# Hybrid decoder trunk, one core: the attention runs without projection work inside it, and the order of work changes at four other places

## The reference

```python
h = rms_norm(x, norm_pre_mix[l])
proj = h @ w_in[l]
p_rwkv, p_nsa, p_swa, p_gate = _split(proj, (RWKV_COLS, NSA_COLS, SWA_COLS, GATE_COLS))
o_rwkv = rwkv7_time_mix(p_rwkv, ...)      # 8 heads of 64, a recurrence over the tokens
o_nsa = nsa_mix(p_nsa, ...)               # compressed, selected and sliding-window branches, 8 heads
o_swa = swa_sink_mix(p_swa, ...)          # window 128, a sink per head
gates = jax.nn.sigmoid(p_gate).reshape(B, T, N_BRANCHES, D)
merged = sum(gates[:, :, i] * (o_i @ w_branch[l, i]) for i in range(3))
x = x + rms_norm(merged @ w_out[l], norm_post_mix[l])
h = rms_norm(x, norm_pre_ffn[l])
f = (silu(h @ ffn_w_gate[l]) * (h @ ffn_w_up[l])) @ ffn_w_down[l]
x = x + rms_norm(f, norm_post_ffn[l])
```

## Time and profile before

| | us |
|---|---|
| median of 3 runs | 1119.35 (1115.24 to 1119.69) |
| profiled execution | 1118.18 |
| its span, first to last instruction | 1116.0 |
| PE busy | 1063.8 (95%) |
| DVE, POOL, ACT busy | 534.5, 505.8, 363.1 |
| granted TensorE clock, mean share of full speed | 0.988 |

### The profile page before, as it was taken

The page is one execution under the profiler, slowest core; times in us unless marked ns, Lnnn a source line. Parts: engine busy times, 40 slices in busy tenths (PEclk is TensorE's granted clock), DMA queues, the critical chain, the costliest instruction groups (busy, mean ns, idle before and its releaser), DMA issues.

```text
span 1116.0 us, 18780 instructions
## 1 busy us (share of the span) xinstructions
PE 1063.8 (95%) x7568; PEld 839.7 (75%) x7568; DVE 534.5 (48%) x909; ACT 363.1 (33%) x708; POOL 505.8 (45%) x428
## 2 busy tenths in 40 slices
PE   5989998999989999999988999999999999999997
PEld 4767777787877667776656877888888888888886
DVE  5774497466465444445544367135445454530004
ACT  4223232321322214444452244444222322221222
POOL 2355544113022347655696544653444444444452
PEclk9999999999999999999998999999999999999999
DMA  7334533002025354221201454812333333333321
GB/s 216 96 89 138 113 88 74 11 13 57 5 59 133 90 123 142 58 58 30 67 20 49 128 174 117 258 40 76 94 94 100 92 109 94 113 95 95 96 93 76
DMA packets 149138, 102.40 MB, mean 92 GB/s; under 512 B 20870, under 2 KB 131728, under 8 KB 149065
## 3 DMA queue, kind: packets, MB, share of 16 engines
q1 hardware_dynamic: 145424, 96.48, 30.0%
q10 hardware_dynamic: 3608, 4.88, 2.0%
q0 software_dynamic: 32, 0.00, 0.0%
HBM read 93.72 MB, written 7.63 MB: 91 GB/s over the span
## 4 chain that ended last, share of the span: by engine, by line
PE 82%; DVE 10%; POOL 3%; issue 1%; ACT 1%; DMA 1%; ACTq 0%; DVEq 0%; POOLq 0%
PE ps L1491 17%; PE ps L1493 15%; PE ps L1492 15%; PE ps L1627 4%; PE ps L1937 4%; PE ps L1938 4%; PE ps L1936 4%; PE ps L1537 3%; PE ps L1788 3%; PE ps L1835 2%; POOL EB L638 1%; DVE XF L1039 1%; PE ps L1858 1%; PE ps L1859 1%; PE ps L1860 1%
## 5 line engine op out<-in xcount | busy, mean ns | idle before, releaser
L577 POOL TENSOR_TENSOR WLO<-WRAW,WHI 128x1024 fp32r<-128x1024 f32 (+1 forms) x129 | 287.7, 2231 | 295.3 <-ACT WHI L690 170.0
L1491 PE MATMUL ps<-HHI,WHI 128*128 128x512 f32 x776 | 319.3, 411 | 8.1 <-DVE GATES L995 5.4
L1492 PE MATMUL ps<-HLO,WHI 128*128 128x512 f32 x776 | 305.5, 394 | 0.0
L1493 PE MATMUL ps<-HHI,WLO 128*128 128x512 f32 x776 | 305.4, 394 | 0.0
L1491 PEld LDWEIGHTS ps<-HHI,WHI 128*128 128x128 f32 x776 | 147.5, 190 | 63.6 <-issue 29.4
L1493 PEld LDWEIGHTS ps<-HHI,WLO 128*128 128x128 f32 x776 | 147.2, 190 | 31.9
L1492 PEld LDWEIGHTS ps<-HLO,WHI 128*128 128x128 f32 x776 | 147.6, 190 | 29.1 <-issue 1.9
L581 POOL CAST WHI<-WRAW 128x256 fp32r<-128x256 f32 (+1 forms) x83 | 48.4, 583 | 192.1 <-PE ps L1493 192.1
L690 ACT ACTIVATE WHI<-WRAW 128x1024 fp32r<-128x1024 f32 (+1 forms) x70 | 63.6, 909 | 161.0 <-PE ps L1493 82.9
L1449 DVE TENSOR_TENSOR FT<-FT 128x512 f32<-128x512 f32 x22 | 51.7, 2348 | 89.0 <-ACT FT L942 89.0
L836 ACT ACTIVATE EB<-EB,MISC 128x257 f32<-128x257 f32 (+5 forms) x96 | 50.7, 530 | 66.7 <-DVE MISC L1337 53.2
(11 more groups left out here) (303 smaller groups left out, 1668.8 us busy)
## 6 DMA issues: line engine op xcount, KB each, us to landing
WRAW<-in_w_in SPq DMA_DIRECT2D x47, 512.0 KB, 4.0
WRAW<-in_w_gate SPq DMA_DIRECT2D x22, 512.0 KB, 3.9
WRAW<-in_w_up SPq DMA_DIRECT2D x22, 512.0 KB, 4.0
WRAW<-in_w_down SPq DMA_DIRECT2D x22, 512.0 KB, 3.9
spilled<-SQ SPq DMA_DIRECT2D x21, 256.0 KB, 2.3
WRAW<-in_w_in SPq DMA_DIRECT2D x16, 256.0 KB, 3.8
WRAW<-in_w_branch SPq DMA_DIRECT2D x32, 128.0 KB, 2.9
WRAW<-in_w_out SPq DMA_DIRECT2D x8, 512.0 KB, 4.2
```

Source lines behind the costliest of these rows:

```text
L577: return pool.tensor_tensor(lo[:, 0:chunks, :], WRAW[:, n % NRAW, 0:chunks, :], hi[:, 0:chunks, :].bitcast(F32), ALU.subtract)
L1491: pe.matmul(dst, WHI[:, s, k, :], hi, start=start, stop=False)
L1492: pe.matmul(dst, WHI[:, s, k, :], lo, start=False, stop=False)
L1493: return pe.matmul(dst, WLO[:, s, k, :], hi, start=False, stop=stop)
```

## The change

- `FILL`: the fill before the first RWKV pass goes from 16 to 20 chunks, the one that opens each pass from 2 to 5, the last before the attention from 4 to 7. No fill is left inside the attention. Behind it come `PT_TAIL`, three fills of one tile each, and the rest. That makes 192 chunks (24 tiles) before and 120 chunks (15 tiles) behind.
- Attention: scores alternate between `R[0]`, `R[1]` and `DB[0]`, `DB[1]`, so they wait for step n - 2; transposes stand three steps behind the scores and PV four; `EB` has four buffers. Before its first step PE waits for the evacuation of the last projection tile. POOL's cutting of weights into pieces is gone; two tiles are prepared before the attention, the others behind it.
- Start: x in four tiles of 128 tokens, three of them ahead of the first weight tile, one between the first two; constants issued by SP and not by ACT; transposes into eight banks; squares summed over the free dimension of x on ACT and DVE, one root and reciprocal of 128x4, spread by diagonals and the ones-matmul; weight tile 1's high part on POOL, weight tile 0's ahead of the copies on ACT. The root's table is the one loaded first.
- `compress_low(0)` stands before `compress_in(1)`, `compress_low(1)` stays.
- Behind the attention one tile is evacuated before each four `OLO` operations.
- Several semaphores are merged into `norm_std`; their waits are the same.

```diff
@@ -136,7 +136,7 @@
-POOL_HI = list(range(NS0 + 4, MERGE0))
+POOL_HI = [1] + list(range(NS0 + 4, MERGE0))
@@ -188,11 +188,11 @@
 FILL = []
-PT_UP = len(FILL); FILL += [4, 4, 8, 8, 16]
+PT_UP = len(FILL); FILL += [4, 4, 8, 8, 20]
 PT_CP = []
 for _cp in range(4):
-    PT_CP.append(len(FILL)); FILL += [2, 4, 4] + [0] * 4 + [1, 1, 1, 1, 1, 4]
-PT_GN = len(FILL); FILL += [3, 6, 6, 6, 4, 4, 8, 8, 4, 4, 4]
+    PT_CP.append(len(FILL)); FILL += [5, 4, 4] + [0] * 4 + [1, 1, 1, 1, 1, 4]
+PT_GN = len(FILL); FILL += [3, 6, 6, 6, 4, 4, 8, 8, 4, 4, 7]
@@ -203,9 +203,9 @@
 NST = len(STEPS)
-PT_ATT = len(FILL); FILL += [2] * NSA_STEPS + [1] * (NST - NSA_STEPS) + [0] * 3
 _ends = np.cumsum([j[3] for j in JOBS[NS0:MERGE0]])
-PT_SPLIT = len(FILL); FILL += [_ends[-1] - sum(FILL)]
+PT_TAIL = len(FILL); FILL += [8, 8, 8]
+FILL += [_ends[-1] - sum(FILL)]
 DONE = []
@@ -214,8 +214,8 @@
 FILLED = np.cumsum(FILL)
-ATT_JOB = NS0 + int(np.sum(_ends - 8 < FILLED[PT_ATT - 1] + 8))
-assert all(j[3] == 8 for j in JOBS[ATT_JOB - 1:MERGE0])
+ATT_JOB = NS0 + int(FILLED[PT_TAIL - 1]) // 8
+assert FILLED[PT_TAIL - 1] % 8 == 0 and ATT_JOB > SW0 + 6
@@ -302,8 +302,8 @@
-    EB = at("EB", 50, [P, 3, 2, T])
-    PTB = at("PTB", 62, [P, 2, 2, T])
+    EB = at("EB", 50, [P, 4, 2, T])
+    PTB = at("PTB", 66, [P, 2, 2, T])
@@ -382,6 +382,9 @@
+    def score_bank(n, g):
+        return (R[g], DB[g])[n % 2]
...
     def out_bank(t, dh):
...
@@ -510,16 +514,28 @@
+    selt = con[0:NH, CON["selT"]:CON["selT"] + 4 * P].rearrange("h (m p) -> h m p", m=4)
...
     block = nc.Block()
...
         def _(sp):
-            for c in range(2):
-                sp.dma_start(XTOK0[:, :, 512 * c:512 * c + 512], x.rearrange("(t p) d -> p t d", p=P)[:, :, 512 * c:512 * c + 512])\
-                    .then_inc((x_in, xtok_in)[c], 16)
+            def x_tile(t):
+                sp.dma_start(XTOK0[:, t, :], x[t * P:(t + 1) * P, :]).then_inc(x_in[t], 16)
...
+            for t in range(3):
+                x_tile(t)
             for n in range(FF0):
-                if n < 2:
-                    sp.wait_ge((x_in, xtok_in)[n], 16)
+                if n == 1:
+                    x_tile(3)
+                if n == 2:
+                    sp.dma_start(HOT[:, :], hot).then_inc(hot_in, 16)
+                    sp.dma_start(SNK, bass.AP(sinks.tensor, 0, [[0, P], [1, NH]])).then_inc(hot_in, 16)
+                    sp.dma_start(MASK[:, :], con[:, NCONP:NCON]).then_inc(hot_in, 16)
+                if n == 3:
+                    sp.dma_start(SELT[0][:, :, :], selt).then_inc(selt_in, 16)
+                    sp.dma_start(WA[0:64, :], w2).then_inc(wsmall_in, 16)
+                    sp.dma_start(WA[64:128, :], a2).then_inc(wsmall_in, 16)
                 if n - 4 in SPILLED:
@@ -588,37 +604,15 @@
-            for n in range(ATT_JOB):
+            for n in range(ATT_JOB + 1):
                 whole_tile(n)
...
-            split = {"at": int(_ends[ATT_JOB - NS0 - 1]), "pieces": 0}
...
-            def split_upto(count):
...
-                while split["at"] < min(count, int(_ends[-1])):
-                    n = NS0 + int(np.sum(_ends <= split["at"]))
...
-                    lo = pool.tensor_tensor(WLO[:, slot_of(n), k:k + 2, :], WRAW[:, n % NRAW, k:k + 2, :],
-                                            WHI[:, slot_of(n), k:k + 2, :].bitcast(F32), ALU.subtract)
...
             pool.memset(ECB[:, :, :, :], 0.0).then_inc(zero_ok, 1)
...
+            whole_tile(ATT_JOB + 1)
...
@@ -638,21 +632,21 @@
-            for n in range(NST + 3):
+            for n in range(NST + 1):
                 if n < NST and STEPS[n][0] == "swa":
-                    pool.wait_ge(p_T, n - 2)
-                    pool.tensor_copy(EB[:, n % 3, :, keys_of(n):keys_of(n) + 1],
+                    pool.wait_ge(p_T, n - 3)
+                    pool.tensor_copy(EB[:, n % 4, :, keys_of(n):keys_of(n) + 1],
                                      NSNK[:, STEPS[n][2]:NH:4].unsqueeze(2)).then_inc(snk_ok, 1)
-                if 1 <= n < NST + 1:
+                if n >= 1:
                     weigh(n - 1)
-                split_upto(int(FILLED[PT_ATT + n]) + 8)
-            split_upto(int(_ends[-1]))
+            for n in range(ATT_JOB + 2, MERGE0):
+                whole_tile(n)
...
                 if u == 2:
-                    pool.wait_ge(xtok_in, 32)
+                    pool.wait_ge(xtok_in, 16)
                     for n in range(8):
@@ -678,40 +672,35 @@
             act.wait_ge(eps_ok, 1)
-            act.activation(MISC[:, 70:72], EPSC, ACT.Square)
+            act.activation(MISC[:, 70:72], EPSC, ACT.Sqrt)
...
                     act.wait_ge(dense_done, slot_free(n))
-                if n == MERGE0:
+                if n in (2, MERGE0):
                     act.wait_ge(w_hi, n)
...
+            def x_square(t):
+                act.wait_ge(x_in[t], 16)
+                act.activation(SQ[:, :, :].rearrange("p a t -> p (a t)"), XTOK0[:, t, :], ACT.Square,
+                               accum_out=XSS[:, t:t + 1]).then_inc(xsq_ok, 1)
...
+            x_square(0)
+            act.wait_ge(xsq_ok, 1)
+            x_square(2)
+            hi_part(0)
             act.wait_ge(prow_ok, 2)
...
                 act.wait_ge(xT_done, k + 1)
-                act.activation(HHI[:, k, :], R[k % 4][:, :], ACT.Identity, scale=par("g_pre_mix", k))
-                if k >= 2:
-                    act.wait_ge(xsum_ok, k - 1)
-                act.activation(SQ[:, k % 2, :], R[k % 4][:, :], ACT.Square).then_inc(xsq_ok, 1)
-                if k == 3:
-                    hi_part(0)
...
-                    act.dma_start(MASK[:, :], con[:, NCONP:NCON]).then_inc(hot_in, 16)
-                    act.dma_start(WA[0:64, :], w2).then_inc(wsmall_in, 16)
-                    act.dma_start(WA[64:128, :], a2).then_inc(wsmall_in, 16)
-                    selt = con[0:NH, CON["selT"]:CON["selT"] + 4 * P].rearrange("h (m p) -> h m p", m=4)
-                    act.dma_start(SELT[0][:, :, :], selt).then_inc(selt_in, 16)
-                    act.dma_start(HOT[:, :], hot).then_inc(hot_in, 16)
-                    act.dma_start(SNK, bass.AP(sinks.tensor, 0, [[0, P], [1, NH]])).then_inc(hot_in, 16)
-            hi_part(1)
-            act.wait_ge(norm_ss, 1)
-            act.wait_ge(eps_ok, 1)
-            act.activation(SQ[:, 0, :], R[4][:, :], ACT.Sqrt, scale=1.0 / D, bias=EPSC[:, 0:1]).then_inc(norm_std, 1)
+                act.activation(HHI[:, k, :], psum[k][:, :], ACT.Identity, scale=par("g_pre_mix", k)).then_inc(xhigh_ok, 1)
+            act.wait_ge(xsq_ok, 2)
+            act.wait_ge(xsum_ok, 2)
+            act.activation(XRINV, XSS, ACT.Sqrt, scale=1.0 / D, bias=EPSC[:, 0:1]).then_inc(norm_std, 1)
...
@@ -848,13 +837,13 @@
-            for n in range(NST + 4):
+            for n in range(NST + 5):
                 if n < NST:
                     exps(n)
-                if 2 <= n < NST + 2:
-                    second_half(n - 2)
-                if n - 4 in GROUP_END:
-                    group_out(GROUP_END.index(n - 4))
+                if 3 <= n < NST + 3:
+                    second_half(n - 3)
+                if n - 5 in GROUP_END:
+                    group_out(GROUP_END.index(n - 5))
...
@@ -1056,22 +1045,28 @@
+            def x_square(t):
+                dve.wait_ge(x_in[t], 16)
+                dve.tensor_tensor_reduce(TMP[:, 0:2, :].rearrange("p a t -> p (a t)"), XTOK0[:, t, :], XTOK0[:, t, :],
+                                         1.0, 0.0, ALU.mult, ALU.add, XSS[:, t:t + 1]).then_inc(xsum_ok, 1)
...
+            x_square(1)
             dve.wait_ge(prow_T, 1)
-            dve.tensor_copy(PARC[:, 0:NPAR1], R[4][:, 0:NPAR1]).then_inc(prow_ok, 1)
-            dve.tensor_copy(PARC[:, NPAR1:NPAR1 + NPAR2], R[5][:, 0:NPAR2]).then_inc(prow_ok, 1)
+            dve.tensor_copy(PARC[:, 0:NPAR1], R[5][:, 0:NPAR1]).then_inc(prow_ok, 1)
+            dve.tensor_copy(PARC[:, NPAR1:NPAR1 + NPAR2], R[5][:, P:P + NPAR2]).then_inc(prow_ok, 1)
             dve.wait_ge(prow_ok, 2)
...
             for k in range(KC):
-                dve.wait_ge(xsq_ok, k + 1)
-                dve.scalar_tensor_tensor(out=HLO[:, k, :], in0=R[k % 4][:, :], scalar=par("g_pre_mix", k),
+                dve.wait_ge(xhigh_ok, k + 1)
+                dve.scalar_tensor_tensor(out=HLO[:, k, :], in0=psum[k][:, :], scalar=par("g_pre_mix", k),
                                          in1=HHI[:, k, :].bitcast(F32), op0=ALU.mult, op1=ALU.subtract).then_inc(xlo_ok, 1)
-                if k == 0:
-                    dve.tensor_copy(SSUM[:, :], SQ[:, 0, :]).then_inc(xsum_ok, 1)
-                else:
-                    dve.wait_ge(xsum_ok, k)
-                    dve.tensor_tensor(SSUM[:, :], SSUM[:, :], SQ[:, k % 2, :], ALU.add).then_inc(xsum_ok, 1)
+            dve.wait_ge(xsum_ok, 1)
+            x_square(3)
             dve.wait_ge(norm_std, 1)
-            link(dve.reciprocal(RINV[:, :], SQ[:, 0, :]))
+            link(dve.reciprocal(XRINV, XRINV))
```

(72 more changed lines are left out.)

68 lines of the change are left out of this document (27 added, 41 removed).

## The result

The changed kernel takes 1104.34 us in the median of nine runs (1102.53 to 1110.49), the kernel before 1118.91 in nine runs beside them; the ratio is 0.9898 with a 95% interval of 0.9871 to 0.9925. It is faster by 1.0% (11.4 us), which is 43% of the gain forecast (26.7 us); the medians lie 14.6 us apart, 55% of it. The time is within the range given. The profiled execution took 1104.16 (span 1102.4).

What follows compares the result with a forecast made beforehand. PE, busy 95% of the span, was taken to bound the kernel, with waits and low clock to win back. 8.5 + 4.4 + 7.3 + 0 - 0.9 + 7.4 = 26.7 off 1118.2 gave 1091.5 profiled, 1092.5 median; range 1083 to 1107.

Steps and rivals of the forecast that it cites:

- XLO term: Moving XF0's low part earlier gains 4.4 us (2.0 to 5.4): 3.7 wait, less 1.0 late weight, plus 1.7 low clock.
- RWKV stage: 19 more projection chunks before the attention cover AR and ST waits and a low-clock stretch: 7.3 us gained (4 to 9).
- I take 0: Attention without fill: no net gain or loss, between 11.6 us gained and 12 lost.
- Rival 1: Attention bound by a chain of several engines, 0.25 us per step and more: 12 us lost, 1104; chance 0.13.
- Point (d): SWA steps: POOL repeats every 1.93 us against PE's 1.74, its last product ending about 4.9 us later than PE needs.
- Half a chance of 1.7: Attention's start: PE's 2.9 us of idleness may bring one low-clock stretch; counted as -0.9 us.
- the sum said 112.2: Attention's cost in us: 101.3 of PE work, 2.9 start idleness, 0.6 evacuation wait, 2.5 short steps, 4.9 POOL in SWA.
- Start: Kernel start, up to the third weight tile: it starts at 27.8 instead of 36.64; 8.5 us taken (5.5 to 10.5).
- new wait of 1.2: RWKV stage, third pass: a tile ends exactly at the last fill's end, so AR brings a new 1.2 us wait.
- Behind the attention: OLO operations split among the evacuations: 5.4 us wait and 2.0 of low clock go, 7.4 gained (6.5 to 7.5).
- The rule on bank cycling: Trainium skill: cycling PSUM banks each iteration with short PE idle spells can make the clock swing between its two levels.
- Rival 2: Clock drops in the attention and stays down; at two thirds of the stage 38 us are lost: 1130; chance 0.05.

Runs made afterwards that it cites:

- second experiment: Changed kernel with ACT's copy of the transposed weights (step n - 3) issued ahead of the exps of step n; 1096.82 us, 7.5 less.
- two-edit kernel: Changed kernel with ACT's copy ahead of the exps and one projection tile in the attention's first six steps; 1092.59 us, 11.8 less.
- third experiment: Changed kernel with one projection tile in the attention's first six steps, last evacuation awaited only ahead of the second score product; 1098.32 us, 6.0 less.
- x_high late: Changed kernel with ACT making the high part of XF1 one dense tile later; 1105.49 us against 1104.34.
- fill-back kernel: Changed kernel with the whole attention of the kernel before put back, 88 projection chunks inside; 1098.97 us, 5.4 less.
- last experiment: Kernel with copy first, head fill and later XF1 high part, every RWKV-stage tile end one chunk earlier; 1090.45 us against 1090.17.
- two steps behind: Two-edit kernel with transposes two steps behind the scores and PV three, not three and four; 1106.80 us, 14.2 more.
- fourth experiment: Changed kernel with ACT making the high part of XF1 behind that of the next dense tile; 1105.49 us against 1104.34.

## Why the prediction was right and where it failed

The profiled execution lies 12.7 us above its forecast (1104.16 against 1091.5), 13.0 by the marks on PE's timeline. Of these 8.1 are in the attention, 3.6 in the XLO term, 1.6 in a stretch not spoken of, 1.3 in the start, 0.2 behind the attention; gains of 0.8 and 0.95 more than forecast (RWKV stage, the stage behind it) stand against them.

**The failed step** is the term for the attention, "I take 0", with -0.9 for the clock: it measured -9.0, clock included. Two of its parts were mis-sized.

The first is ACT's copy. Rival 1 was dismissed on sums of engine time per step ("some 2.1 of PE's 3.05"), and the waiting of an in-order queue was left out: ACT's copy stands behind exps that wait for POOL. What stood in its place is 9.2 us of waits in the trace, and 7.5 us of the median when the copy goes first, some 2.2 of them by the clock (estimate, second experiment). Point (d) looked only for POOL as releaser. POOL's step of 1.93 us came once the copy stood first (nine steps in a row in the two-edit kernel); in the changed kernel the last SWA steps take 1.92, 2.14 and 2.40 us in turn. Rival 1 was the right mechanism, and its sign came, over 120 us with copies as releasers. That its 1104 is the median measured is luck: it stands for 12 us lost in the attention and nothing elsewhere, where 9.0 were lost there and the rest with XLO and at the start.

The second is the head. "Half a chance of 1.7" was two stretches of 6.8 us at 1.2 GHz, worth some 4.6 us (estimate, from the third experiment), and 27.3 us of it in the execution of x_high late. I had 2.9 us of idleness as one wait and 0.6 for the evacuation; they came as 1.7 and 0.3, and 0.9, with small matmuls between. A tile of fill there gave 6.0 us.

With both taken away the attention costs 111.6 us (two edits) where the sum said 112.2. That flatters the sum: the head fill covers the 2.9 and 0.6 as well, so that like with like is 108.7 against 111.6.

**Start**: 7.2 against 8.5. Tile 0 starts at 14.48 and ends at 21.20, 6.7 us where the plain rate gives 5.4: its first matmuls stand 0.43 apart and not 0.225, the pace of the lower clock. The changed kernel's window from 13.6 to 17.0 shows a granted clock of 1.00, but that trace holds no record of the clock ahead of 17.0. In seven of the twelve kernels of the experiments the record reaches further back, and each has 3.4 us at 1.2 GHz that begin between 12.0 and 14.7; their matmuls too stand 0.43 apart until its end. This is x_high late:

```profile
12.90:16.20 3.30, 3.15 (x11) 2.47 (x10) 2.75 (x5) 3.30 (x7) 3.22 (x3) 0.50 1.08 336
```

The fill-back kernel's trace has full clock from 10.3 on, and its tile 0 took 5.6. So the 1.3 us are most likely one low-clock stretch, which the forecast had in its lower bound and not in its value; the third tile started between 28.14 and 30.00 in these twelve. The order of events was as worked out.

**XLO**: 0.8 in the trace, against 4.4, and nothing in the medians when its order alone was put back (that trace, of the slowest of its five runs, is 2.6 longer there, 1.7 of it by the clock). The wait went, but "1.0 us (0 to 1.8)" for the weight that is late next was 3.2, and the low clock stayed. What holds this place is not XLO's order but the XF1 operations ahead of everything else in DVE's queue, 8.23 us for four of them, which x_high(1) and the weight's high part follow, and DVE's mixing too: with x_high(1) moved the wait went on to DVE. That move gave 2.4 us in the median, of which the traces put 0.9 at these waits.

**RWKV stage**: 8.1 against 7.3. The new wait of 1.2 in the third pass came as 1.3, and taking 16 of the 19 chunks out again cost 6.6. The counting of chunks against a chain of known length held, save that I followed only one of the chain's links (AR); the last experiment shows that the others (ST, AM) meet tile ends too.

**Behind the attention**: 7.2 against 7.4, and that is luck, for the cause was another. The interleaving of OLO gave 0.7 of it in the median, within the spread. What is left is that two whole tiles now stand ahead of the first evacuation, and that POOL is idle beside the block; neither was undone by itself.

**Not foreseen**: 6.8 us at 1.2 GHz from 116.0 after the sums over KK, where before 3.4 stood at 125.9 (1.6 lost). The prediction named three low stretches; the trace before has three more of 3.4 us, at 20.1, at 125.9 and at 385.3. The cause of this one was not isolated; every kernel here has a stretch of 3.4 or 6.8 at that place.

**The rule on bank cycling** ("TensorE: Matmul & The Clock Gate", "A second HAM failure mode: psum-queue depth-cycling" in the Trainium skill) is borne out in part. The head of the attention, with small matmuls and gaps, swings between both levels, for 6.8 to 27.3 us. From 435 on the same cycling with 0.4 to 0.6 of idling in the short steps stays at 1.00, and so does the kernel two steps behind, with its 27 waits of 0.63 us on average. Rival 2 had its direction, though not its extent; eight chunks of dense work in the head end it. Whether the banks have a part in it beside the idle times no run here shows.

## What to carry to other kernels

Filler taken out of a latency-bound stage, one in which each step waits for a chain through several engines, must be paid for link by link: walk each engine's queue in program order and ask, for every copy that frees a bank, which waiting instruction stands in front of it. Sum the waits of a line over all its steps, since twenty of 0.5 us cost more than one of five. A few chunks of dense work belong at the entry of such a stage, where the pipeline is still filling, even if the rest runs better without. And a wait that was removed is not shown to be worth its length, nor a gain to come from the edit meant for it, until that edit alone has been undone.

## What the runs showed of the hardware

- The share of time at 1.2 GHz differs between executions of one kernel, and with it the time: mean granted clock 0.979 to 0.989 and 1110.5 to 1102.5 us in nine runs of the changed kernel, 0.989 to 0.992 and 1095.2 to 1092.1 us in five of the two-edit kernel.
- What a microsecond at 1.2 GHz costs depends on how full PE is: in the small, gappy steps at the head of the attention 13.7 us more cost 4.6, a third of a microsecond each; in dense projection work matmuls of 512 columns stand 0.43 us apart and not 0.225, about half a microsecond each.
- Four DVE operations on 64x496 elements took 8.23 us, partly beside POOL's work, and 10.19 in the fourth experiment; the shortest of them took 1.00 each.
- A granted clock of 1.00 in a window can also mean that the trace has no record of the clock there: in the changed kernel's window from 13.6 to 17.0 matmuls stand 0.43 us apart from 15.5 to 16.8 at a shown 1.00, and the trace's first record is at 17.0.
